# Windowed attention on TensorE with padded 128-row operands instead of array tiles, and norms emitted at other places

## What is computed

```python
s_band = jnp.einsum('bnqkgd,bnskd->bnkgqs', qb, k_band) + bias_band   # previous + current block of 128
s_meta = jnp.einsum('bnqkgd,bmkd->bnkgqm', qb, km) + bias_meta
p = jax.nn.softmax(jnp.concatenate([s_meta, s_band, sink_b], axis=-1), axis=-1)
o_r = (jnp.einsum('bnkgqm,bmkd->bnqkgd', p_meta, vm)
       + jnp.einsum('bnkgqs,bnskd->bnqkgd', p_band, v_band))
...
h = h + m
h = h + swiglu(rms_norm(h, norm_ffn[i]), ffn_w_gate[i], ffn_w_up[i], ffn_w_down[i])
```

## Time and profile before

| | us |
|---|---|
| median of 3 runs | 2873.87 |
| lowest, highest | 2853.85, 3209.59 |
| the profiled execution: time | 2855.66 |
| its span on the slowest core | 2854.1 |
| spans of the eight cores | 2845.9 to 2854.1 |
| mean granted TensorE clock | 0.988 to 0.990 |

### The profile page before, as it was taken

One profiled execution on the slowest core, in us unless ns is written; L12 is line 12 of the kernel. 1 busy time (PEld: TensorE's weight loads), 2 busy tenths in 40 slices (PEclk: granted clock), 3 DMA queues, 4 the chain that ended last, 5 costly groups with the idle time before them and its releaser, 6 DMA issues.

```text
span 2854.1 us, 52443 instructions; the slowest of 8 cores (2845.9 to 2854.1 us)
## 1 busy us (share of the span) xinstructions
PE 2708.6 (95%) x18178; PEld 1673.3 (59%) x18178; DVE 1512.2 (53%) x3107; ACT 954.8 (33%) x1904; POOL 280.1 (10%) x532
## 2 busy tenths in 40 slices
PE   5779999998999999999999999999999999999997
PEld 2446655555566566656566666666556775555564
DVE  4655455546444734646647667335544655553444
ACT  4544344431111213211322223124334544442222
POOL 0000101000011011101111111111001111000110
PEclk9899999999999999999999999999999999999998
DMA  8435545555566566655566576756456675555663
GB/s 230 66 60 92 98 82 101 86 86 89 97 106 103 94 112 113 102 98 97 92 110 103 93 122 103 119 98 111 84 93 105 113 126 89 97 92 89 101 123 99
DMA packets 81235, 290.83 MB, mean 102 GB/s; under 512 B 9748, under 2 KB 11732, under 8 KB 80212
## 3 DMA queue, kind: packets, MB, share of 16 engines
q0 software_dynamic: 76032, 265.85, 56.5%
q1 hardware_dynamic: 4948, 21.64, 2.2%
HBM read 544.87 MB, written 8.39 MB: 194 GB/s over the span
## 4 chain that ended last, share of the span: by engine, by line
PE 84%; DVE 7%; issue 4%; DMA 3%; ACT 2%; DVEq 0%; SPq 0%; ACTq 0%; POOL 0%; POOLq 0%
PE ps L126 84%; DVE sb_scr L126 2%; DMA sb_h<-x 1%; DVE sb_qt L126 1%; DVE sb_Pt L126 1%; DMA sb_ring<-attn_q 1%; DVE sb_abf L126 1%; DVE sb_abm L126 0%; ACT sb_sqf L126 0%; DMA out<-sb_abm 0%; DVE sb_gbf L126 0%; DVE sb_sqf L126 0%; ACT sb_rden L126 0%; DVE sb_sq L126 0%; DVEq L124 0%
## 5 line engine op out<-in xcount | busy, mean ns | idle before, releaser
L126 PE MATMUL ps<-sb_abf,sb_ring 128*128 128x384 bf16 (+2 forms) x8608 | 1344.6, 318 | 11.2 <-DVE sb_abf L126 4.0
L126 PEld LDWEIGHTS ps<-sb_abf,sb_ring 128*128 128x128 bf16 x8608 | 843.6, 98 | 494.5 <-issue 24.4
L126 PE MATMUL ps<-sb_gbf,sb_ring 128*128 128x384 bf16 (+2 forms) x4352 | 711.8, 317 | 3.2 <-DVE sb_gbf L126 3.2
L126 DVE TENSOR_TENSOR sb_gbf<-ps,sb_sgt 128x384 bf16<-128x384 f32 (+2 forms) x528 | 281.6, 534 | 730.5 <-PE ps L126 615.8
L126 PEld LDWEIGHTS ps<-sb_gbf,sb_ring 128*128 128x128 bf16 x4352 | 410.2, 98 | 262.4 <-issue 43.3
L126 ACT ACTIVATE sb_sgt<-ps 128x384 f32<-128x384 f32 (+2 forms) x528 | 248.0, 472 | 871.5 <-PE ps L126 784.9
L126 DVE TENSOR_TENSOR sb_h<-ps,sb_h 128x384 f32<-128x384 f32 (+2 forms) x624 | 330.6, 533 | 277.5 <-PE ps L126 274.3
L126 PE MATMUL ps<-sb_abm,sb_ring 128*128 128x384 bf16 (+2 forms) x1952 | 321.7, 322 | 18.5 <-DVE sb_qt L126 11.3
L126 PEld LDWEIGHTS ps<-sb_abm,sb_ring 128*128 128x128 bf16 x1952 | 189.1, 98 | 141.0 <-issue 38.6
L126 POOL DMA_DIRECT2D sb_ring<-ffn_gu x264 | 140.4, 532 | 1273.7 <-PE ps L126 1264.3
L126 ACT ACTIVATE sb_sqf<-sb_h 128x384 f32<-128x384 f32 (+2 forms) x304 | 142.4, 494 | 264.3 <-DVE sb_sqf L126 220.0
(11 more groups left out here) (88 smaller groups left out, 1272.3 us busy)
## 6 DMA issues: line engine op xcount, KB each, us to landing
sb_ring<-ffn_gu POOLq DMA_DIRECT2D x264, 512.0 KB, 5.3
sb_ring<-ffn_dn POOLq DMA_DIRECT2D x96, 448.0 KB, 4.8
sb_ring<-ffn_dn POOLq DMA_DIRECT2D x48, 512.0 KB, 5.8
sb_ring<-conv_in POOLq DMA_DIRECT2D x36, 512.0 KB, 5.4
sb_ring<-attn_q POOLq DMA_DIRECT2D x24, 512.0 KB, 6.2
sb_ring<-attn_o POOLq DMA_DIRECT2D x24, 512.0 KB, 5.3
sb_h<-x SPq DMA_DIRECT2D x4, 1536.0 KB, 31.2
sb_ring<-conv_out POOLq DMA_DIRECT2D x12, 512.0 KB, 5.3
```

Source lines behind the costliest of these rows:

```text
L126: ins = getattr(e, name)(*a_, **kw_)
```

## The change

Six things change.
1. `kt` gets a second copy dimension: each head has its own 128-row keys, its 64 rows filled and the other 64 zero. `va`, `vbe`, `vbo` hold 192 columns a pair: head, 64 zeros, head; a slice of 128 from 0 or from 64 is one head's values with zeros for the other. `onesz` is built alike. Scores use all 128 rows, values and sums all 128 columns, and both heads accumulate in one region (`start` at the first of four, `stop` at the last). The keys are written by two instructions of 64 partitions.
2. Where the two score banks are neighbours and the item is an ordinary one, one exponential and one product cover both banks.
3. `ring` has five slots. In the first pair the query weights of the second tile are taken in the order 2 to 7, 0, 1, and unit 0 is loaded again. `vm` moves into `rden`, which has one buffer; `attbv` holds one layer and is loaded again for layer 3; `pic` shares its memory.
4. `norm_ffn` gives statistics and scales of each tile apart. `ffn` lays the statistics of tile 0 beside the second half of `proj_out`, where attention items stand; in front of convolution inputs and of layer 3 the whole norm moves into the feed-forward ahead.
5. These norms ahead of convolution inputs of passes 1 and 2 are made with `quads`.
6. `final` stores four quarters a tile, each with its own key.

```diff
-NSLOT = 6
+NSLOT = 5
...
-    kt = sb("kt", [128, 2, KTC], BF16)
...
+    kt = sb("kt", [128, 2, 2, KTC], BF16)
...
+    va, vbe, vbo = [sb(x, [128, NVS, 2, 192], BF16) for x in ("va", "vbe", "vbo")]
...
+    P.op("dve", _I.memset(onesz[:], 1.0), writes=[B("onesz")])
+    P.op("dve", _I.memset(onesz[:, 64:128], 0.0), writes=[B("onesz")])
...
-            return kt[hf * 64:(hf + 1) * 64, pr, c:c + 128]
+            return kt[:, pr, hf, c:c + 128]
...
-                                         rhs=qx[hf * 64:(hf + 1) * 64, 4 * pr:4 * pr + 4, qc:qc + nq], start=True, stop=True),
+                                         rhs=qx[:, 4 * pr:4 * pr + 4, qc:qc + nq], start=True, stop=True),
...
+            st["both"] = nq == 64 and sb_[1] == sb_[0] + 1 and not (p == 0 and jb in (0, 1))
+            if st["both"]:
+                S = psum[:, sb_[0] * 512:(sb_[0] + 2) * 512]
+                keys = [psb[x] for x in sb_]
+                P.op("act", _I.activation(out=S, in_=S, func=AF.Exp, scale=0.125), reads=keys, writes=keys)
...
+            if st["both"]:
+                e0 = (par * 4 + 2 * pr) * 512
+                P.op("dve", _I.tensor_tensor(out=Pt[:, pb[0]:pb[0] + 2, :], in0=psum[:, sb_[0] * 512:(sb_[0] + 2) * 512].rearrange("p (a c) -> p a c", a=2),
+                                             in1=eb[:, e0:e0 + 1024].rearrange("p (a c) -> p a c", a=2), op=ALU.mult),
...
+                            w, rk = onesz[:, hf * 64:hf * 64 + 128], [B("onesz")]
...
+                            w, rk = v[:, slot, pr, hf * 64:hf * 64 + 128], [B(name, slot)]
+                        P.op("pe", _I.matmul(ps[ob][:, what * 256:what * 256 + W], lhsT=w,
+                                             rhs=Pt[:, st["pb"][hf], ch * 256:ch * 256 + W],
+                                             start=(hf == 0 and ch == 0), stop=(hf == 1 and ch == 1)),
...
+                out = mixer_out(i + 1)
+                (s0, e0), (s1, e1) = norm_ffn(*lp(i + 1), quads=lp(i + 2)[0] != 1)
+                _run(out[0:KC])
+                _run(out[KC:], s0)
+                _run(more, e0 + s1 + e1, 0.9)
...
+            full = i + 2 < N and lp(i + 2)[0] % 3 == 2
+            (s0, e0), (s1, e1) = norm_ffn(*lp(i + 1), quads=not full)
+            mid = dn[0] + gu[1] + dn[1] + gu[2]
...
+                _run(mid, prep[0] + prep[1] + s0 + s1)
+                _run(dn[2], e0 + e1)
+            _run(more)
...
+    (s0, e0), (s1, e1) = norm_ffn(0, 0)
+    _run(out0[KC:], s0)
+    _run(keys, e0 + s1 + e1, 0.9)
```

More of the change, by code:

```diff
@@ L267, in build @@
     psc = sb("psc", [128, KC])
-    pic = sb("pic", [128, KC * NMETA])
+    pic = attbv[:, 0:KC * NMETA]
     NSQ = 4
@@ L774, in attn_in @@
             for ti, t in enumerate(tiles):
-                part = [(8 * t[1], lambda c=c, t=t: qstep(c, t)) for c in range(KC)]
+                part = [(8 * t[1], lambda c=c, t=t: qstep(c, t)) for c in (range(KC) if ti == 0 else (2, 3, 4, 5, 6, 7, 0, 1))]
+                if ti == 1:
+                    part.insert(6, (0, lambda: slot.pop(0)))
                 for pr in range(2):
@@ L1015, in prelude @@
                 claim("scr", [B("zt"), B("cacc")])
+                P.op("sp", _I.dma_start(out=pic, in_=pic_d), writes=[B("attbv")], dma="pic")
         def step(c, ti, t):
@@ L1204, in ffn @@
         items = attn_items(*lp(i + 1)) if has_core(i + 1) else []
-        early = i + 1 < N and not mixer_in(i + 2)
-        nf = norm_ffn(*lp(i + 1), quads=False) if early else []
+        more = i + 1 < N and mixer_in(i + 2)
         gu = [ffn_gu(l, p, g) for g in range(3)]
```

217 lines of the change are left out of this document (110 added, 107 removed).

## The result

| | us |
|---|---|
| changed kernel, median of 20 runs | 2873.69 |
| kernel before, median of 20 runs beside it | 2854.42 |
| ratio, 95% interval | 1.0065, 1.005 to 1.008 |
| changed, profiled execution: span of core 0 | 2872.1 |
| spans of the eight cores | 2866.6 to 2872.1 |

The change makes the kernel 0.65% slower, some 18.5 us. (Some executions of any kernel here are disturbed: one die runs at a lower granted clock and the time is longer, as in one of the three behind the 2873.87 us shown before; the median over twenty is 2854.42, the ratios use undisturbed executions alone, and so the two medians that look alike are not a tie.) Against the profiled execution of before the sum said +10 us; the spans differ by 18.0.

What follows compares the result with a forecast made beforehand. TensorE is busy 95% of the span, so its own work and its waits set the time. Terms 37.6 + 6 + 2 - 9.5 - 14 - 5 - 7 = +10 us on the profiled 2855.7 give 2866 us, range 2842 to 2892.

Steps and rivals of the forecast that it cites:

- padding: Attention matmuls on TensorE: full-size scores, values and sums cost +0.285 us an item, 132 items, +37.6 us (33 to 45).
- joint exponentials: Attention on ACT and DVE: longer chain uncovered at about 20 places at 0.3 us, +6 us (0 to 15).
- keys of pass 1: Layer 0, keys of pass 1: moved norms shorten PE's waits, 33.35 to about 24 us, -9.5 us (-5 to -12).
- convolution inputs: Three convolution input stretches: norm work moved out of them cuts PE's idle time, together -14 us (-8 to -18).
- starts of attention stages: Attention stage starts: a third of the 16 us left of waits for `sb_sq` goes, -5 us (-2 to -8).
- final stores: Tail: quarter stores with their own keys spare scales the wait for the store DMA, -7 us (-5 to -8).
- ring, start-up, copies: Five slots cost 0; doubled zeroing, reloads, half-height key copies and longer value copies: together +2 us (0 to 5).
- the waits swallow the padding: Rival, attention: added matmuls fall into PE's waits for `sb_qt` and `sb_Pt`, costing 10 us, total 2838 us; chance 0.08.
- padding at full price: Rival, attention: the 0.1 us at shape changes stays, 0.65 us an item, 86 us in all, total 2914 us; chance 0.05.
- where scales collide with the gate products on DVE: Convolution inputs: PE's idle time put down to norm scales on DVE; -5 us first stretch, -7.5 us the two others.
- the -3.9 us net: Second and third convolution inputs: twelve of sixteen totals go in each thanks to quads, 24 x 0.16 = -3.9 us.
- the signs named ahead: Trace checks: blocks 0.44 and 0.87 us, no `sb_sq` wait over 1 us at keys, PE full in later convolution inputs, others.

Runs made afterwards that it cites:

- the first experiment: Changed kernel with both attention matmul kinds (scores, and values and sums) back on array tiles, all else kept: 2840.09 us, ratio 0.9955 to the kernel before.
- The score experiment: Changed kernel with only the score matmuls back on array tiles, values and sums still padded: 2881.22 us, ratio 1.0079 to the kernel before.
- order alone: Kernel before with only the change's new order of norms (`norm_ffn`, `ffn` and its start): 2829.89 us, ratio 0.9913.
- U, C, B: Each convolution step's three ring groups reversed from B, C, U: on the kernel before 2830.04 us, ratio 0.9915; on the changed kernel 2850.67 us, 0.9986.

## Why the prediction was right and wrong

The measured 2873.69 us lies in the range and 8 us above the forecast of 2866, but the gain or tie that 2866 suggests beside the median shown does not hold: the kernel is slower by 0.65%, where my sum against the profiled run gave 0.35%. The steps:

| step | predicted | measured |
|---|---|---|
| padding | +37.6 | +31 (ratio), +34 (spans) |
| joint exponentials | +6 | +6 to +8 alone, +13 with the padding |
| keys of pass 1 (with the projection ahead) | -9.5 | -10.0 alone, -8.0 in the changed kernel |
| convolution inputs | -14 | -6.2 alone, -4.6 in the changed kernel; +1.3 in the stages between and behind |
| starts of attention stages | -5 | -9.5 |
| final stores | -7 | -8.2 (tail), -9 to -10 (times) |
| ring, start-up, copies | +2 | 0 slots, 0 zeroing, +6 to +8 copies alone (to number 576) |
| sum | +10 | +18.5 |

**Padding: right in mechanism, a little high.** Blocks of 0.43 and 0.87 us and 0.29 us an item came as read; the twenty items of pass 0 cost nothing, since PE waits there anyway. What it did not see is that the scores are free and values and sums carry it all. The rival "the waits swallow the padding" falls with the first experiment; "padding at full price", which the 2x of the Trainium skill's page TensorEngine Tiling (Array Packing) would give, asks for 86 us where 31 to 34 were measured. (It is the third of the rivals listed, where the text on the 2x calls it the second.) The score experiment agrees with its rule on draining (Tiling Modes, Key Properties): two tiled pairs of 256 columns between full-width matmuls gain nothing at all.

**Convolution inputs: wrong, and the largest miss.** The step that failed is "where scales collide with the gate products on DVE", priced at -5 and -7.5 us of waits. The rows showed PE idle while VectorE had work of both kinds, and I took the norm for the cause because the diff moves it. In the first stage the norm's departure gives 0 of the 5 us. In the other two it gives 2.8 and 3.5 us, where 11.4 were written for both, and most of that is the term that stood beside it, PE's own time for the totals that leave (2.3 and 2.6 us; four a stage come back elsewhere, so the -3.9 us net was right). PE's waits there shrink only from 3.1 to 2.4 us and from 2.8 to 1.6 (kernel before, order alone), 1.9 us where 7.5 were written. The waits come from the order of the three groups in a step: with U, C, B and the whole norm still beside them they are gone from the second and third stage. The trace of before allowed the check that I left out: the chain from the last group to the bank's release against the matmuls that stand between. That chain needs no norm to be longer than the 2.6 us of matmuls between.

**Joint exponentials: right alone, wrong in company.** The estimate looked at the tiled kernel, where it holds (6 to 8 us). In the changed kernel the values also change their order, head by head, and the separate form would have used that. Edit by edit the costs were judged on the kernel before, though one edit made another dearer.

**Start-up and copies: mis-sized, for the wrong reason.** I counted the zeroing (nothing) and let the key copies pass as "two half-height ones", as if half height were half price. Alone they cost 5.8 us to number 576 against the profile of before (202.9 to 197.2) and 8 against the kernel with five slots (194.9).

**Starts and stores: too small.** A third of the waits for `sb_sq` was an arbitrary share; it was 9.5 us. The tail gave 8.2 by the stages, 9 to 10 by the times.

The misses upward (convolution 9 to 11, joint 7, start and copies some 4) are 20 to 22 us, those downward (padding 4 to 7, starts 4.5, stores 1 to 3, keys 0.5) 10 to 15; the two leave 5 to 12, and +10 and +18.5 differ by 8.5. So the forecast lands as near as it does because misses of both signs cancel, in part by luck.

**Of the signs named ahead,** four came: score and value blocks as long as said, full pace behind them, no wait for `out` at the end, and POOL waiting 2526.3 us for PE. Three did not. At the keys a wait of 3.61 us for `sb_sq` is left, and the granted clock from 175 to 200 us is 0.86; PE still waits 2.7 and 2.0 us in the second and third convolution inputs; and waits for `sb_Pt` grew from 12.8 to 20.0 us. The joint form is what they grew by (7.3 us without it).

## What to carry to other kernels

When a group of matmuls waits for a bank, follow the chain that releases that bank and set it against the matmuls that stand in between, before blaming whatever else runs on the engine; then issue first the group whose result is needed first and released first. On ScalarE, look for a way to split along the columns before splitting along the partitions: here each half of a split by partitions took the time of the whole. A merged instruction is worth judging by what could have started on its first half, and again after every other edit that changes who waits for it.

## What the runs showed of the hardware

- Sixty-four partitions of a ScalarE copy take the time of 128: 577 and 582 ns at 384 columns.
- Two pairs of 64-row matmuls of 256 columns, in place of four of 128 rows, between full-width matmuls: -0.3 us on 24 items, so nothing. Both kinds tiled, with eight 64-column weights in place of eight of 128: 0.29 us less an item; the eight alone bring as much in the whole time (31 us).
- One instruction may read two neighbouring PSUM banks: 1008 ns on ScalarE and 1214 ns on VectorE for 1024 columns, where 512 take 576 and 683. Both save about 0.15 us on a pair.
- Most stages with PE as the bound repeat to 0.1 us over eight cores (192.95 to 192.98 us for the 24 items of pass 1), and so show differences of 0.3 us that a total with 5 us of spread at the start hides.
